# Window attention: the order of maxima and low halves, and shared value products for the previous chunk's keys

## The chip, the cores and the metric

One core of a Trainium2 chip runs one launch of the whole kernel. The metric is the device time of that launch in microseconds. The profile is of one further execution of the same program.

## The reference, cut to what matters

The program is one encoder block: projections with rotary positions, two attentions (a windowed one, A, and a differential one, B), gates and merge, a layer norm, and a mixture of experts. The change is in the windowed attention A alone. Its reference, for 2048 positions in chunks of 64, 8 query heads, 2 key heads, head size 64:

```python
qc = q.reshape(b, nc, CHUNK, A_KV_HEADS, grp, d)
kb = window_chunks(k, 2)   # keys of the chunk before and of the own chunk
vb = window_chunks(v, 2)
sc = einsum('bnqkgd,bnjkd->bnkgqj', qc, kb) * d ** -0.5
sc = where(valid, sc, NEG_INF)            # chunk 0 has no chunk before it
m = maximum(max(sc, -1), sink)            # one learned sink per head
e = exp(sc - m)
p = e / (sum(e, -1) + exp(sink - m))
o = einsum('bnkgqj,bnjkd->bnqkgd', p, vb)
```

## The kernel before, in words

The program runs in stages, each with a barrier behind it: weights and projection (j), differential attention (b), window attention (a, `window_attention_phase`, L480 to L770), merge (m), routing (r), experts (e), combination (o). Names of tiles in the profile carry the stage's letter: `a_tp` is `tp` of the window attention.

Float32 values are kept as a high part in fp32r and a low part, the remainder. So q and k are loaded as 64 rows of high parts on 64 rows of low parts; `kh` and `kl` hold the high and the low parts of the keys on both halves, and two products over 128 rows give all four terms.

A tile is 128 queries (two chunks). It needs 192 keys: the 64 of the chunk behind the tile and its own 128. A **unit** is one tile and one key head, which serves four query heads; there are UNITS = 32. In a unit the engines do this:

- TensorE, scores (L643 to L653): for each of 4 heads three products of 192 columns into a PSUM bank pair `bank[g]`: q with `kh`, q with `kl`, and a mask product that adds a large negative number where a chunk may not look. 12 matmuls.
- VectorE, maxima (L727 to L737): one reduction over the four heads' scores, then three small instructions up to `nb`, the negated maximum.
- ScalarE, exponentials (L698 to L703): four activations from PSUM into `pr` with their sums, and `se` for the sinks.
- TensorE, turn (L675 to L678): for each head two transposes of `pr`, the tile's own 128 keys into `tc` and the 64 behind it into `tp`. 8 matmuls. `tp` and `tc` are single buffers in PSUM.
- ScalarE copies them out as high parts `tph`, `tch` (L708, L709); VectorE makes the low halves `tpl`, `tcl` (L749, L751).
- TensorE, values (L655 to L669): for each head four products into `po[g]`, two over the tile's own 128 keys (128 and 64 columns) and two over the 64 keys behind it (64 and 128 columns; weights of 64 rows). 16 matmuls.
- VectorE scales by the inverse denominator (L744), GpSimd adds the two halves (L610), SP stores (L559). ScalarE and GpSimd also split one slice of the merge stage's weights a tile (L714, L603), which GpSimd's queue loads (L616).

The order of the work is written by hand, engine by engine. TensorE begins with the scores of units 0 and 1, and then in unit n does turn(n), scores(n+2), values(n-1). VectorE in unit n does the low halves of n, the inverse of n, maxima(n+2), and the scaling of n-1. ScalarE does copies(n), then exponentials(n+1). Four units are a turn of a loop (L626 to L634). turn(n) waits for the exponentials of n and, as `t_lo` starts at 2, for the low halves of n-1 (L672, L674). SP's queue loads q and k two tiles ahead, V one tile ahead, and stores (L561 to L585), in that order.

The core of TensorE's unit:

```python
pe.wait_ge(exped, n + 1)
pe.wait_ge(t_lo, 2 * n + 2)
# transposes of unit n
scores_of(k + u, 1 - u, g, 0)      # unit n + 2
values_of(n - 1, ...)
```

Of the kernel before, what the change touches and what calls it, by code (L numbers as in the profile page):

```python
# [21 lines left out]
P = 128  # L22
# [457 lines left out]
def window_attention_phase(nc, sinks, ident, qk_hi, qk_lo, v_hi, v_lo, oa, w_slices, w_hi, w_lo):  # L480
# [11 lines left out]
    UNITS = A_KV * NT  # L492
    with Phase(nc, "a") as ph:
# [18 lines left out]
        mask_f = ph.sb("mask_f", [P, P + 2 * W])  # L512
        mask = ph.sb("mask", [P, P + 2 * W], F32R)
        bank = [ph.ps(f"s{g}", [P, GH // 2, BANK]) for g in range(A_KV)]
        tp = ph.ps("tp", [CHUNK, GH, P])
# [7 lines left out]
        w_in, w_his, w_los = ph.sems("w_in", 2), ph.sem("w_his"), ph.sem("w_los")  # L523
        block = ph.block()

        def score(g, j):
            return bank[g][:, j // 2, (j % 2) * W:(j % 2 + 1) * W]

        @block.sync
        def _(sp):  # L530
            sp.dma_start(sink[:], sinks.rearrange("a (g h) -> a g h", g=A_KV).to_broadcast([P, A_KV, GH])).then_inc(sink_in, 16)
            for u in range(2):
                sp.sem_inc(stored[u], 16)


            def load_qk(t, u):
                cols = bass.ts(t, P)
                first = isinstance(t, int) and t == 0
                for half, src in ((0, qk_hi), (1, qk_lo)):
                    rows = slice(half * HD, (half + 1) * HD)  # L540
                    sp.dma_start(f(qs[rows, u]), src[0:4, :, cols].rearrange("c (b p) n -> p (c b) n", b=2)).then_inc(qk_loaded[u], 16)
                    for dst, ksrc in ((kh, qk_hi), (kl, qk_lo)):
                        k = ksrc[4].rearrange("(g p) n -> p g n", g=A_KV)
                        if first:
                            sp.dma_start(f(dst[rows, u, :, 0:CHUNK]), k[:, :, 0:CHUNK]).then_inc(stand_in, 16)
                            sp.dma_start(f(dst[rows, u, :, CHUNK:W]), k[:, :, cols]).then_inc(qk_loaded[u], 16)
                        else:
                            sp.dma_start(f(dst[rows, u]), k[:, :, bass.ds(t * P - CHUNK, W)]).then_inc(qk_loaded[u], 16)

            def load_v(t, u):  # L550
                first = isinstance(t, int) and t == 0
                tile, rows = (slice(0, 1), slice(0, CHUNK)) if first else (bass.ds(t - 1, 1), slice(CHUNK, P))
                for half, src in enumerate((v_hi, v_lo)):
                    for dst, at in ((vp, (tile, rows)), (vc, (bass.ds(t, 1), slice(0, P)))):
                        sp.dma_start(f(dst[:, u, :, half, :]), src[at[0], at[1], 0:A_K].rearrange("a p (g d) -> p (a g) d", g=A_KV)).then_inc(v_loaded[u], 16)

            def store(t, u):
                sp.wait_ge(added, 2 * t + 2)
                sp.dma_start(oa[bass.ts(t, P), :], o[:, u].rearrange("p g h d -> p (g h d)")).then_inc(stored[u], 16)  # L559

            def step(s, u):  # L561

                sp.wait_ge(scores, 2 * s + 2)
                load_qk(s + 2, u)

                sp.wait_ge(pv, 2 * s)
                load_v(s + 1, 1 - u)
                store(s - 1, 1 - u)

            load_qk(0, 0)  # L570
            load_v(0, 0)
            load_qk(1, 1)
            load_v(1, 1)
            sp.wait_ge(scores, 2)
            load_qk(2, 0)
            with sp.Fori(0, NT // 2 - 2) as i:
                step(2 * i + 1, 1)
                step(2 * i + 2, 0)
            step(NT - 3, 1)
            sp.wait_ge(pv, 2 * (NT - 2))  # L580
            load_v(NT - 1, 1)
            for t in range(NT - 3, NT):
                store(t, t % 2)
            for u in range(2):
                sp.wait_ge(stored[u], 16 * (NT // 2 + 1))  # L585

        @block.gpsimd
        def _(pool):


            nc.gpsimd.memset(mask_f[:], 0.0).then_inc(mask_step, 1)
# [3 lines left out]
            for first in range(2):  # L595
                m0 = P + W * first
                nc.gpsimd.memset(mask_f[0:1, m0 + P:m0 + W], NEG).then_inc(mask_step, 1)
                nc.gpsimd.memset(mask_f[32:33, m0:m0 + CHUNK], NEG).then_inc(mask_step, 1)
            nc.gpsimd.memset(mask_f[0:1, P + W:P + W + CHUNK], NEG).then_inc(mask_step, 1)
# [5 lines left out]
            def sum_parts(t):  # L605

                pool.wait_ge(stored[t % 2], 16 * (t // 2 + 1))
                for g in range(A_KV):
                    pool.wait_ge(scaled, 2 * t + g + 3)
# [13 lines left out]

        def over_tiles(eng, unit):  # L626
            for g in range(A_KV):
                unit(g, 0, 0, g, n0=True if g == 0 else False, tail=False)
            with eng.Fori(0, NT // 2 - 1) as i:
                for w in range(2):  # L630
                    for g in range(A_KV):
                        unit(2 * (2 * i + 1 + w) + g, i + w, 1 - w, g, n0=False, tail=False)
            for g in range(A_KV):
                unit(UNITS - 2 + g, NT // 2 - 1, 1, g, n0=False, tail=True)  # L634

        def tile_of(k, u):
            return 2 * k + u

        @block.tensor
        def _(pe):  # L640
            pe.wait_ge(mask_step, 9)

            def scores_of(k, u, g, first):  # L643

                if g == 0:
                    pe.wait_ge(qk_loaded[u], 6 * 16 * (k + 1))
                for j in range(GH):
                    q = qs[:, u, GH * g + j, :]
                    nc.tensor.matmul(score(g, j), q, kh[:, u, g, :], start=True, stop=False)
                    nc.tensor.matmul(score(g, j), q, kl[:, u, g, :], start=False, stop=False)  # L650
                    m0 = P + W * first
                    last = nc.tensor.matmul(score(g, j), mask[:, 0:P], mask[:, m0:m0 + W], start=False, stop=True)
                last.then_inc(scores, 1)  # L653

            def values_of(n, k, u, g):  # L655

                pe.wait_ge(t_lo, 2 * n + 4)

                pe.wait_ge(scaled, n + 1)
                if g == 0:  # L660
                    pe.wait_ge(v_loaded[u], 4 * 16 * (k + 1))
                for j in range(GH):

                    both, high = po[g][:, j].rearrange("p s d -> p (s d)"), po[g][:, j, 0, :]
                    nc.tensor.matmul(both, tch[:, g, j, :], vc[:, u, g].rearrange("p s d -> p (s d)"), start=True, stop=False)
                    nc.tensor.matmul(high, tcl[:, g, j, :], vc[:, u, g, 0, :], start=False, stop=False)
                    nc.tensor.matmul(high, tpl[:, g, j, :], vp[:, u, g, 0, :], start=False, stop=False)
                    last = nc.tensor.matmul(both, tph[:, g, j, :], vp[:, u, g].rearrange("p s d -> p (s d)"), start=False, stop=True)
                last.then_inc(pv, 1)  # L669

            def unit(n, k, u, g, n0, tail):
                pe.wait_ge(exped, n + 1)  # L672

                pe.wait_ge(t_lo, 2 * n + 2)  # L674
                for j in range(GH):  # L675
                    nc.tensor.transpose(tc[:, j, :], pr[:, g, j, CHUNK:W], ident[:])
                    last = nc.tensor.transpose(tp[:, j, :], pr[:, g, j, 0:CHUNK], ident[:])
                last.then_inc(turned, 1)  # L678
                if not tail:

                    scores_of(k + u, 1 - u, g, 0)
                if not n0:

                    if g:
                        values_of(n - 1, k, u, 0)
                    else:
                        values_of(n - 1, k - (1 - u), 1 - u, 1)


            pe.wait_ge(stand_in, 4 * 16)  # L690
            scores_of(0, 0, 0, 1)
            scores_of(0, 0, 1, 1)
            over_tiles(pe, unit)
            values_of(UNITS - 1, NT // 2 - 1, 1, 1)

        @block.scalar
        def _(act):
            def exps(n, g):  # L698
                act.wait_ge(maxed, 3 * n + 3)
                for j in range(GH):  # L700
                    nc.scalar.activation(pr[:, g, j, :], score(g, j), ACT.Exp, bias=nb[:, g, j:j + 1], scale=SCALE,
# [3 lines left out]
            def unit(n, k, u, g, n0, tail):  # L705

# [3 lines left out]
                if not (tail and g):  # L710
                    exps(n + 1, 1 - g)
                if g:
                    act.wait_ge(w_in[u], 16 * (k + 1))
                    nc.scalar.activation(w_hi[:, bass.ds(tile_of(k, u), 1), :], raw[:, u:u + 1, :], ACT.Copy).then_inc(w_his, 1)  # L714

            exps(0, 0)
            over_tiles(act, unit)

        @block.vector
        def _(dve):  # L720
            dve.sem_inc(t_lo, 2)
            dve.sem_inc(scaled, 2)
            dve.wait_ge(mask_step, 8)
# [3 lines left out]
            def maxima(n, g):  # L727
# [11 lines left out]
            def scale(n, k, u, g):  # L739
                dve.wait_ge(pv, n + 1)  # L740
                if not isinstance(n, int) or n >= 2:
# [5 lines left out]
            def unit(n, k, u, g, n0, tail):  # L747
                dve.wait_ge(t_hi, 2 * n + 1)
# [1509 lines left out]
```

## Time and profile before

| | |
|---|---|
| median of 3 runs | 3273.95 us (3270.92 to 3274.72) |
| profiled execution | 3276.61 us |
| its span, first to last instruction | 3275.1 us |
| mean granted TensorE clock | 0.898 |
| TensorE matmuls busy | 2722.8 us (83%) |
| VectorE busy | 1660.9 us (51%) |
| ScalarE busy | 1140.0 us (35%) |
| GpSimd busy | 794.2 us (24%) |
| window attention | 1400.27 to 1626.46 us of the span |

The profile is one execution. Times of instructions are counted from the span's start. PE is TensorE's matmuls and PEld its weight loads, which overlap them; DVE is VectorE, ACT ScalarE, POOL GpSimd, SP SyncE and SPq its queue of DMA issues. The end of a matmul in the profile is modelled, so its duration exceeds the time to the next one's start; the cost of one in a dense run is read from start to start. PEclk is the granted clock as a share of full speed, 2.4 GHz; its two levels are 1.0 and 0.5 (2.4 and 1.2 GHz), and a mean over a stretch lies between them. A bracket behind a row gives how long the engine had been idle, and what ended that.

### The profile page before, as it was taken

What the parts mean: (1) busy time and instruction counts of PE and PEld (TensorE: products, weight loads), DVE (VectorE), ACT (ScalarE), POOL (GpSimd) and SP (SyncE); (2) the same over time, 40 slices, a digit from 0 to 9 for tenths busy, and PEclk for the clock granted to TensorE, in tenths of its full rate; (3) what the DMA queues carried; (4) which work ended last, traced back from release to release, by engine and by line L of the source; (5) the groups of instructions that cost most, each with busy time, mean ns of one, the idle gap of its engine ahead of it and who ended that gap; (6) DMA issues with size and microseconds to landing.
All of it is one profiled execution on the core that took longest, in us unless ns stands there. A gap on an engine that the chain in (4) does not pass through costs nothing. (4 is left out here: it accounts for less than half of the span.)

```text
span 3275.1 us, 48737 instructions
## 1 busy us (share of the span) xinstructions
PE 2722.8 (83%) x14667; PEld 2336.4 (71%) x14668; DVE 1660.9 (51%) x3065; ACT 1140.0 (35%) x1888; POOL 794.2 (24%) x630
## 2 busy tenths in 40 slices
PE   2999993996978969889889997529999999999910
PEld 2888882885867858689778886317888888888810
DVE  5333332655636546345444443426565556666568
ACT  2111111433424434344311110216465455656522
POOL 2111110000000000023213232043343233324346
PEclk9999995997988979967699999759999999999965
DMA  4444437356373363355333331538687577768566
GB/s 148 144 144 144 144 132 184 109 157 178 118 213 122 134 186 134 112 150 139 102 119 119 105 119 41 182 116 326 240 303 283 215 285 282 285 234 314 212 222 220
DMA packets 278694, 582.78 MB, mean 178 GB/s; under 512 B 41536, under 2 KB 136000, under 8 KB 275520
## 3 DMA queue, kind: packets, MB, share of 16 engines
q1 hardware_dynamic: 184464, 437.26, 39.9%
q10 hardware_dynamic: 76944, 88.62, 7.7%
q0 software_dynamic: 17184, 55.60, 5.3%
q8 instruction: 57, 0.93, 0.1%
q14 instruction: 45, 0.37, 0.0%
HBM read 451.31 MB, written 130.07 MB: 178 GB/s over the span
## 5 line engine op out<-in xcount | busy, mean ns | idle before, releaser
L1776 DVE TENSOR_TENSOR e_wl<-rw_raw,e_wh 128x1024 fp32r<-128x1024 f32 (+1 forms) x288 | 374.2, 1343 | 46.4 <-ACT e_wh L1922 46.4
L1922 ACT ACTIVATE e_wh<-rw_raw 128x1024 fp32r<-128x1024 f32 (+1 forms) x384 | 377.9, 1053 | 17.3 <-DMA rw_raw<-w_gate_up 13.3
L1776 POOL TENSOR_TENSOR e_wl<-rw_raw,e_wh 128x1024 f32 (+1 forms) x96 | 238.8, 2512 | 298.2 <-ACT e_wh L1922 298.1
L301 PE MATMUL j_pg<-qkv_w_hi,j_xh 128*128 128x512 f32 (+1 forms) x640 | 242.4, 379 | 1.5 <-DVE j_xl L419 1.5
L303 PE MATMUL j_pg<-qkv_w_lo,j_xh 128*128 128x512 f32 (+1 forms) x640 | 237.3, 371 | 0.0
L302 PE MATMUL j_pg<-qkv_w_hi,j_xl 128*128 128x512 f32 (+1 forms) x640 | 236.4, 369 | 0.0
L1871 PE MATMUL e_p_up<-e_wh,e_xh 128*128 128x256 f32 (+1 forms) x784 | 225.4, 288 | 0.0
L1873 PE MATMUL e_p_up<-e_wl,e_xh 128*128 128x256 f32 (+1 forms) x784 | 221.7, 283 | 0.0
L1872 PE MATMUL e_p_up<-e_wh,e_xl 128*128 128x256 f32 (+1 forms) x784 | 221.7, 283 | 0.0
L931 POOL TENSOR_TENSOR b_o<-b_parts 128x128 f32<-128x128 f32 x64 | 30.9, 482 | 758.3 <-ACT b_parts L1044 758.3
L983 PE MATMUL b_pg<-b_g_wh,b_g_xh 128*128 128x512 f32 x512 | 213.6, 417 | 1.4 <-DVE b_g_out L1158 0.8
L1106 DVE TENSOR_SCALAR_CACHE_REDUCE b_sc<-b_s 128x512 f32<-128x512 f32 (+3 forms) x320 | 179.4, 605 | 49.2 <-PE b_s L958 36.1
L983 PE MATMUL b_pg<-b_g_wl,b_g_xh 128*128 128x512 f32 x512 | 203.5, 398 | 0.0
L983 PE MATMUL b_pg<-b_g_wh,b_g_xl 128*128 128x512 f32 x512 | 202.2, 395 | 0.0
L1036 ACT ACTIVATE b_th<-b_t 128x512 fp32r<-128x512 f32 (+3 forms) x160 | 85.3, 533 | 290.8 <-PE b_t L968 290.8
L955 PE MATMUL b_s<-b_kh,b_qs 128*128 128x512 f32 (+3 forms) x320 | 134.7, 421 | 55.0 <-issue 29.4
L1029 ACT ACTIVATE b_sc<-b_sc,b_nb 128x128 f32<-128x128 f32 (+15 forms) x128 | 153.0, 1195 | 54.1 <-DVE b_nb L1117 54.1
L1883 PE MATMUL e_py<-e_wh,e_hh 128*128 128x512 f32 x392 | 164.2, 419 | 0.0
L356 POOL TENSOR_TENSOR j_turned<-j_by_cos,j_by_sin 128x512 f32<-128x512 f32 x64 | 68.8, 1086 | 391.7 <-DVE j_by_sin L443 391.7
L968 PE MATMUL b_t<-ident,b_at 128*128 128x128 f32 x544 | 90.3, 282 | 86.0 <-DVE b_at L1139 86.0
L1871 PE MATMUL e_p_gate<-e_wh,e_xh 128*128 (+1 forms) x392 | 155.1, 396 | 5.9 <-DVE e_wl L1776 3.1
L438 DVE TENSOR_TENSOR j_by_cos<-j_pg,qkv_cos 128x512 f32<-128x512 f32 x64 | 37.7, 589 | 234.0 <-DMA v_lo<-j_vl 145.3
(313 smaller groups left out, 7307.6 us busy)
## 6 DMA issues: line engine op xcount, KB each, us to landing
rw_raw<-w_gate_up SPq DMA_DIRECT2D x256, 512.0 KB, 6.4
rw_raw<-w_down SPq DMA_DIRECT2D x128, 512.0 KB, 7.9
b_g_xh<-xt_hi SPq DMA_DIRECT2D x64, 512.0 KB, 4.0
b_g_xl<-xt_lo SPq DMA_DIRECT2D x64, 512.0 KB, 5.0
ys<-e_yo ACTq DMA_DIRECT2D x49, 512.0 KB, 7.6
gates<-b_g_out ACTq DMA_DIRECT2D x64, 256.0 KB, 4.4
m_gt<-gates SPq DMA_DIRECT2D x16, 1024.0 KB, 8.1
qk_hi<-j_qkh ACTq DMA_DIRECT2D x16, 832.0 KB, 4.5
```

The lines of the kernel that those rows point to most:

```text
L301: nc.tensor.matmul(out, xh[:, u, ks], w_hi[:, k, cs], start=(k == 0), stop=False)
L302: nc.tensor.matmul(out, xl[:, u, ks], w_hi[:, k, cs], start=False, stop=False)
L303: last = nc.tensor.matmul(out, xh[:, u, ks], w_lo[:, k, cs], start=False, stop=(k == KD - 1))
L983: last = nc.tensor.matmul(pg[:], x_side, w_side, start=(q == 0), stop=(q == PASSES - 1))
L1029: nc.scalar.activation(sc[:, u, m, 0:L], sc[:, u, m, 0:L], ACT.Exp, bias=nb[:, u, m:m + 1], scale=SCALE, accum_out=sums[:, u, m:m + 1]).th ...
L1106: nc.vector.tensor_scalar(sc[:, u, m, ks], bank[n % 4][:, 0:ks.stop - ks.start], 1.0, NEG, ALU.mult, ALU.max, accum_out=mx[:, u, m, g:g + ...
L1776: (nc.gpsimd if done is w_lo_pool else nc.vector).tensor_tensor(wl[:, slot(e, s), :], raw[:, s:s + 1, :], f(wh[:, slot(e, s), :]), ALU.sub ...
L1871: nc.tensor.matmul(out[:, 0:js.stop - js.start], xh[:, at], hi, start=(k == 0), stop=False)
L1872: nc.tensor.matmul(out[:, 0:js.stop - js.start], xl[:, at], hi, start=False, stop=False)
L1873: last = nc.tensor.matmul(out[:, 0:js.stop - js.start], xh[:, at], lo, start=False, stop=(k == KD - 1))
L1883: nc.tensor.matmul(py[:, js], hh[:, at], wh[:, n, js], start=(k == 0), stop=False)
L1922: nc.scalar.activation(wh[:, slot(e, s), :], raw[:, s:s + 1, :], ACT.Copy).then_inc(w_hi, 1)
```

## The change

TensorE now issues, in unit n, scores(n+1), turn(n), values(n-1), and the scores of 0 and 1 ahead of all. VectorE issues inverse(n-1), maxima(n+1), low halves(n-1), scaling(n-2). ScalarE issues exponentials(n+1), then copies(n). `pr` holds two heads side by side so that the 64 keys behind the tile of an even and of an odd head are neighbours: one transpose turns both (2 instead of 4 for `tp`), and one pair of products over 128 rows, against `vz`, whose rows hold V of those 64 keys twice with zeros elsewhere, gives both heads' part (256 columns). For that layout the scores of even heads are written in swapped pieces of 128 and 64 columns. The loops over tiles are written out.

```diff
-        vp = ph.sb("vp", [CHUNK, 2, A_KV, 2, HD], F32R)
+        vz = ph.sb("vz", [P, 2, A_KV, 2, 2, HD], F32R)
-        pr = ph.sb("pr", [P, A_KV, GH, W])
-        tph = ph.sb("tph", [CHUNK, A_KV, GH, P], F32R)
-        tpl = ph.sb("tpl", [CHUNK, A_KV, GH, P], F32R)
+        pr = ph.sb("pr", [P, A_KV, PAIRS, 2 * W])
+        tph = ph.sb("tph", [P, A_KV, PAIRS, P], F32R)
+        tpl = ph.sb("tpl", [P, A_KV, PAIRS, P], F32R)
-        tp = ph.ps("tp", [CHUNK, GH, P])
+        tp = ph.ps("tp", [P, PAIRS, P])
...
+            def load_qk(t):
+                u, cols = t % 2, slice(t * P, (t + 1) * P)
+                if t >= 2:
+                    sp.wait_ge(scores, 2 * t - 2)
...
+            def load_v(t):
+                u = t % 2
+                if t >= 2:
+                    sp.wait_ge(pv, 2 * t - 2)
...
                 for half, src in enumerate((v_hi, v_lo)):
+                    rows = tail[half][:, 0:A_K].rearrange("p (g d) -> p g d", g=A_KV)
+                    for j in range(2):
+                        sp.dma_start(f(vz[j * CHUNK:(j + 1) * CHUNK, u, :, j, half, :]), rows).then_inc(v_loaded[u], 16)
+                    sp.dma_start(f(vc[:, u, :, half, :]), src[t, :, 0:A_K].rearrange("p (g d) -> p g d", g=A_KV)).then_inc(v_loaded[u], 16)
...
+            load_qk(0)
+            sp.wait_ge(v_zeroed, 1)
+            load_v(0)
+            load_qk(1)
+            load_v(1)
+            for t in range(NT):
+                if t + 2 < NT:
+                    load_qk(t + 2)
+                if t and t + 1 < NT:
+                    load_v(t + 1)
+                if t:
+                    store(t - 1)
+            store(NT - 1)
...
         @block.gpsimd
         def _(pool):
+            nc.gpsimd.memset(f(vz[:]), 0.0).then_inc(v_zeroed, 1)
             nc.gpsimd.memset(mask_f[:], 0.0).then_inc(mask_step, 1)
...
         @block.tensor
         def _(pe):
+            def scores_of(n):
+                t, g = n // 2, n % 2
+                u, m0 = t % 2, P + M * (t == 0)
                 if g == 0:
+                    pe.wait_ge(qk_loaded[u], 6 * 16 * (t // 2 + 1))
+                if n >= 2:
+                    pe.wait_ge(exped, n - 1)
                 for j in range(GH):
+                    q, odd = qs[:, u, GH * g + j, :], j % 2
+                    nc.tensor.matmul(score(g, j), mask[:, 0:P], mask[:, m0 + odd * P:m0 + odd * P + W], start=True, stop=False)
+                    if odd:
+                        nc.tensor.matmul(score(g, j), q, kh[:, u, g, :], start=False, stop=False)
+                        last = nc.tensor.matmul(score(g, j), q, kl[:, u, g, :], start=False, stop=True)
+                    else:
+                        for k in (kh, kl):
+                            nc.tensor.matmul(score(g, j)[:, 0:P], q, k[:, u, g, CHUNK:W], start=False, stop=False)
+                            nc.tensor.matmul(score(g, j)[:, P:W], q, k[:, u, g, 0:CHUNK], start=False, stop=(k is kl))
                 last.then_inc(scores, 1)
+            def turn(n):
+                g = n % 2
+                pe.wait_ge(exped, n + 1)
+                if n:
+                    pe.wait_ge(t_lo, 2 * n)
+                for j in range(PAIRS):
+                    nc.tensor.transpose(tp[:, j, :], pr[:, g, j, P:2 * P], ident[:])
+                for j in range(GH):
+                    last = nc.tensor.transpose(tc[:, j, :], here_of(g, j), ident[:])
+                last.then_inc(turned, 1)
+            def values_of(n):
+                t, g = n // 2, n % 2
+                u = t % 2
+                pe.wait_ge(t_lo, 2 * n + 2)
+                if n >= 2:
+                    pe.wait_ge(scaled, n - 1)
                 if g == 0:
+                    pe.wait_ge(v_loaded[u], 6 * 16 * (t // 2 + 1))
+                here, there = vc[:, u, g].rearrange("p s d -> p (s d)"), vz[:, u, g].rearrange("p h s d -> p (h s d)")
+                for pair in range(PAIRS):
+                    both = po[g][:, 2 * pair:2 * pair + 2].rearrange("p h s d -> p (h s d)")
+                    nc.tensor.matmul(both, tph[:, g, pair, :], there, start=True, stop=False)
+                    nc.tensor.matmul(both, tpl[:, g, pair, :], there, start=False, stop=False)
+                    for j in (2 * pair, 2 * pair + 1):
+                        out = po[g][:, j].rearrange("p s d -> p (s d)")
+                        nc.tensor.matmul(out, tch[:, g, j, :], here, start=False, stop=False)
+                        last = nc.tensor.matmul(out, tcl[:, g, j, :], here, start=False, stop=bool(j % 2))
                 last.then_inc(pv, 1)
             pe.wait_ge(stand_in, 4 * 16)
+            scores_of(0)
+            scores_of(1)
+            for n in range(UNITS):
+                if 2 <= n + 1 < UNITS:
+                    scores_of(n + 1)
+                turn(n)
+                if n:
+                    values_of(n - 1)
+            values_of(UNITS - 1)
...
         @block.scalar
         def _(act):
+            exps(0)
+            for n in range(UNITS):
+                if n + 1 < UNITS:
+                    exps(n + 1)
+                copies(n)
+                if n % 2:
+                    k = n // 2
+                    act.wait_ge(w_in[k % 2], 16 * (k // 2 + 1))
+                    nc.scalar.activation(w_hi[:, k, :], raw[:, k % 2, :], ACT.Copy).then_inc(w_his, 1)
         @block.vector
         def _(dve):
+            def lows(n):
+                g = n % 2
+                dve.wait_ge(t_hi, 2 * n + 2)
+                nc.vector.tensor_tensor(tpl[:, g], tp[:], f(tph[:, g]), ALU.subtract).then_inc(t_lo, 1)
+                nc.vector.tensor_tensor(tcl[:, g], tc[:], f(tch[:, g]), ALU.subtract).then_inc(t_lo, 1)
+            maxima(0)
+            for n in range(UNITS):
+                if n:
+                    invert(n - 1)
+                if n + 1 < UNITS:
+                    maxima(n + 1)
+                if n:
+                    lows(n - 1)
+                if n >= 2:
+                    dve.wait_ge(summed, 2 * (n - 1))
+                    scale(n - 2)
+            invert(UNITS - 1)
+            lows(UNITS - 1)
+            dve.wait_ge(summed, 2 * UNITS)
+            scale(UNITS - 2)
+            scale(UNITS - 1)
```

The mask grows by one more block of 128 columns for each of its two forms, for the swapped pieces. GpSimd's and SP's waits for sums and stores count the same events with other offsets. The reduction, the exponentials and the scaling keep their shapes.

## Rows read from the trace of the kernel before

**Rows 1.** The page's busy time of TensorE, its weight loads and the other engines.
```profile
PE 2722.8 (83%) x14667; PEld 2336.4 (71%) x14668; DVE 1660.9 (51%) x3065; ACT 1140.0 (35%) x1888; POOL 794.2 (24%) x630
```

**Rows 2.** Stretches; columns: length, five engines' busy us (instructions), PEclk, DMA share, GB/s.
```profile
1400.00:1627.00 227.00, 223.63 (x1152) 203.86 (x1152) 113.67 (x288) 103.58 (x368) 67.20 (x62) 0.69 0.46 123
1440.00:1600.00 160.00, 160.00 (x844) 146.13 (x843) 83.02 (x211) 75.06 (x268) 50.10 (x46) 0.71 0.52 136
1600.00:1620.00 20.00, 20.00 (x84) 17.61 (x83) 8.02 (x19) 8.48 (x26) 6.37 (x6) 0.52 0.19 63
744.00:788.00 44.00, 19.14 (x68) 16.34 (x69) 17.45 (x64) 12.12 (x31) 2.00 (x4) 0.50 0.82 224
```

**Rows 3.** Order of time, the stage's start; columns: start us, duration us, engine, instruction.
```profile
1387.64 0.53 POOL L591 MEMSET a_mask_f<- 128x512 f32 x1 [7.97 <-POOLq L76]
...
1400.27 0.50 PE L649 MATMUL a_s<-a_kh,a_qs 128*128 128x192 f32 x1 [22.83 <-DMA a_kl<-qk_lo]
...
1402.70 0.41 PE L652 MATMUL a_s<-a_mask 128*128 128x192 f32 x1
...
1405.26 0.41 PE L652 MATMUL a_s<-a_mask 128*128 128x192 f32 x1
...
1405.71 0.96 DVE L729 TENSOR_REDUCE a_mx<-a_s 128x4 f32<-128x768 f32 x1 [1.05 <-PE a_s L652]
...
1406.29 0.21 ACT L703 ACTIVATE a_se<-a_diff 128x4 f32<-128x4 f32 x1
...
1406.56 0.48 PE L676 MATMUL a_tc<-ident,a_pr 128*128 128x128 f32 x1 [0.88 <-ACT a_se L703]
...
1406.98 0.16 DVE L737 TENSOR_SCALAR a_nb<-a_m 128x4 f32<-128x4 f32 x1
```

**Rows 4.** Order of time, the stage's last scaling.
```profile
1625.77 0.69 DVE L744 TENSOR_TENSOR a_parts<-a_o,a_inv 128x512 f32<-128x512 f32 x1 [4.03 <-PE a_o L668]
```

**Rows 5.** Waits in the stage; columns: who for whom, us in total, times, longest.
```profile
ACT a_tph L708 <- PE a_tp L677: 110.3, 32, 5.2
```

**Rows 6.** Order of time, two score products after the clock rose.
```profile
1410.11 0.27 PE L650 MATMUL a_s<-a_kl,a_qs 128*128 128x192 f32 x1
...
1410.22 0.27 PE L652 MATMUL a_s<-a_mask 128*128 128x192 f32 x1
```

**Rows 7.** Order of time, PE in the merge stage: two products of 512 columns.
```profile
1646.94 0.63 PE L1293 MATMUL m_psa<-mw_w_lo,m_abh 128*128 128x512 f32 x1
1647.37 0.63 PE L1291 MATMUL m_psa<-mw_w_hi,m_abh 128*128 128x512 f32 x1
```

**Rows 8.** Order of time, PE: a head's first value product and the next head's.
```profile
1516.76 0.33 PE L665 MATMUL a_o<-a_vc,a_tch 128*128 128x128 f32 x1
...
1517.47 0.33 PE L665 MATMUL a_o<-a_vc,a_tch 128*128 128x128 f32 x1
...
1604.70 0.47 PE L665 MATMUL a_o<-a_vc,a_tch 128*128 128x128 f32 x1
...
1605.88 0.47 PE L665 MATMUL a_o<-a_vc,a_tch 128*128 128x128 f32 x1
```

**Rows 9.** Groups by form in the stage; mean ns of one after the comma.
```profile
L749 DVE TENSOR_TENSOR a_tpl<-a_tp,a_tph 64x512 fp32r<-64x512 f32 x32 | 21.8, 682 | 44.5 <-ACT a_tph L708 44.5
L751 DVE TENSOR_TENSOR a_tcl<-a_tc,a_tch 128x512 fp32r<-128x512 f32 x32 | 21.5, 672 | 0.0
...
L753 DVE TENSOR_TENSOR a_den<-a_sums,a_se 128x4 f32<-128x4 f32 x32 | 4.6, 144 | 0.0
```

**Rows 10.** Waits of SP's queue in the stage.
```profile
SPq L555 <- PE a_o L668: 80.2, 14, 10.1
```

**Rows 11.** Order of time, PE in the routing stage, transposes alone.
```profile
2058.01 3.65 PE L1550 MATMUL r_pt<-ident,r_xin 128*128 128x128 f32 x16 [0.76 <-DVE r_tl L1631]
2062.41 1.07 PE L1550 MATMUL r_pt<-ident,r_xin 128*128 128x128 f32 x8 [0.76 <-DVE r_tl L1631]
```

**Rows 12.** Order of time, PE in the merge stage, after a gap.
```profile
1663.88 1.07 PE L1284 MATMUL m_pt<-ident,m_pa 128*128 128x128 f32 x8 [3.03 <-POOL m_pa L1376]
```

More of the change, by code:

```diff
@@ L492, in window_attention_phase @@
     UNITS = A_KV * NT
+    PAIRS = GH // 2
+    M = W + P
     with Phase(nc, "a") as ph:
@@ L511, in window_attention_phase @@
         raw = ph.sb("raw", [P, 2, D])
-        mask_f = ph.sb("mask_f", [P, P + 2 * W])
-        mask = ph.sb("mask", [P, P + 2 * W], F32R)
+        mask_f = ph.sb("mask_f", [P, P + 2 * M])
+        mask = ph.sb("mask", [P, P + 2 * M], F32R)
         bank = [ph.ps(f"s{g}", [P, GH // 2, BANK]) for g in range(A_KV)]
-        tp = ph.ps("tp", [CHUNK, GH, P])
+        tp = ph.ps("tp", [P, PAIRS, P])
         tc = ph.ps("tc", [P, GH, P])
@@ L531, in _ @@
             sp.dma_start(sink[:], sinks.rearrange("a (g h) -> a g h", g=A_KV).to_broadcast([P, A_KV, GH])).then_inc(sink_in, 16)
[L532 to L538, printed above, removed]
+            def load_qk(t):
+                u, cols = t % 2, slice(t * P, (t + 1) * P)
+                if t >= 2:
+                    sp.wait_ge(scores, 2 * t - 2)
                 for half, src in ((0, qk_hi), (1, qk_lo)):
@@ L543, in load_qk @@
                         k = ksrc[4].rearrange("(g p) n -> p g n", g=A_KV)
-                        if first:
+                        if t == 0:
                             sp.dma_start(f(dst[rows, u, :, 0:CHUNK]), k[:, :, 0:CHUNK]).then_inc(stand_in, 16)
@@ L547, in load_qk @@
                         else:
[L548 to L552, printed above, removed]
-                for half, src in enumerate((v_hi, v_lo)):
-                    for dst, at in ((vp, (tile, rows)), (vc, (bass.ds(t, 1), slice(0, P)))):
-                        sp.dma_start(f(dst[:, u, :, half, :]), src[at[0], at[1], 0:A_K].rearrange("a p (g d) -> p (a g) d", g=A_KV)).then_inc(v_loaded[u], 16)
@@ L573, in _ @@
[L573 to L583, printed above, removed]
+                            sp.dma_start(f(dst[rows, u]), k[:, :, t * P - CHUNK:(t + 1) * P]).then_inc(qk_loaded[u], 16)
@@ L595, in _ @@
             for first in range(2):
[L596 to L599, printed above, removed]
+                m0 = P + M * first
+                nc.gpsimd.memset(mask_f[0:1, m0 + CHUNK:m0 + P], NEG).then_inc(mask_step, 1)
+                nc.gpsimd.memset(mask_f[0:1, m0 + W + CHUNK:m0 + M], NEG).then_inc(mask_step, 1)
+                nc.gpsimd.memset(mask_f[32:33, m0 + P:m0 + W], NEG).then_inc(mask_step, 1)
+            nc.gpsimd.memset(mask_f[0:1, P + M + P:P + M + W], NEG).then_inc(mask_step, 1)
             def low_w(n):
@@ L621, in _ @@
             sum_parts(NT - 1)
[L626 to L634, printed above, removed]
@@ L647, in scores_of @@
                 for j in range(GH):
[L648 to L652, printed above, removed]
-                last.then_inc(scores, 1)
-            def values_of(n, k, u, g):
-                pe.wait_ge(t_lo, 2 * n + 4)
-                pe.wait_ge(scaled, n + 1)
-                if g == 0:
[L661 to L668, printed above, removed]
-                last.then_inc(pv, 1)
@@ L671, in unit @@
[L671 to L687, printed above, removed]
@@ L700, in exps, with copies @@
                 for j in range(GH):
-                    nc.scalar.activation(pr[:, g, j, :], score(g, j), ACT.Exp, bias=nb[:, g, j:j + 1], scale=SCALE,
+                    nc.scalar.activation(pr[:, g, j // 2, (j % 2) * W:(j % 2 + 1) * W], score(g, j), ACT.Exp, bias=nb[:, g, j:j + 1], scale=SCALE,
                                          accum_out=sums[:, g, j:j + 1])
                 nc.scalar.activation(se[:, g, :], diff[:, g, :], ACT.Exp).then_inc(exped, 1)
-            def unit(n, k, u, g, n0, tail):
+            def copies(n):
+                g = n % 2
@@ L709, in unit, with maxima @@
                 nc.scalar.activation(tch[:, g], tc[:], ACT.Copy).then_inc(t_hi, 1)
[L710 to L717, printed above, removed]
+            exps(0)
[7 more added lines that the diff above has]
+                    nc.scalar.activation(w_hi[:, k, :], raw[:, k % 2, :], ACT.Copy).then_inc(w_his, 1)
         @block.vector
         def _(dve):
-            dve.sem_inc(t_lo, 2)
-            dve.sem_inc(scaled, 2)
-            dve.wait_ge(mask_step, 8)
+            dve.wait_ge(mask_step, 10)
             nc.vector.tensor_copy(mask[:], mask_f[:]).then_inc(mask_step, 1)
             dve.wait_ge(sink_in, 16)
-            def maxima(n, g):
+            def maxima(n):
+                g = n % 2
                 dve.wait_ge(scores, n + 1)
@@ L745, in scale, with invert @@
                                         inv[:, g, :].unsqueeze(2).to_broadcast([P, GH, 2 * HD]), ALU.mult).then_inc(scaled, 1)
-            def unit(n, k, u, g, n0, tail):
-                dve.wait_ge(t_hi, 2 * n + 1)
-                nc.vector.tensor_tensor(tpl[:, g], tp[:], f(tph[:, g]), ALU.subtract).then_inc(t_lo, 1)
-                dve.wait_ge(t_hi, 2 * n + 2)
-                nc.vector.tensor_tensor(tcl[:, g], tc[:], f(tch[:, g]), ALU.subtract).then_inc(t_lo, 1)
+            def invert(n):
+                g = n % 2
                 dve.wait_ge(exped, n + 1)
@@ L755, in unit @@
                 nc.vector.reciprocal(inv[:, g, :], den[:, g, :]).then_inc(summed, 1)
[L756 to L768 removed]
+            def lows(n):
+                g = n % 2
+                dve.wait_ge(t_hi, 2 * n + 2)
[9 more added lines that the diff above has]
+                    lows(n - 1)
+                if n >= 2:
+                    dve.wait_ge(summed, 2 * (n - 1))
+                    scale(n - 2)
+            invert(UNITS - 1)
+            lows(UNITS - 1)
             dve.wait_ge(summed, 2 * UNITS)
[L770 removed]
+            scale(UNITS - 2)
+            scale(UNITS - 1)
 def diff_attention_phase(nc, w_in, b_gate, xt_hi, xt_lo, gates, lambdas, ident, qk_hi, qk_lo, v_hi, v_lo, ob):
```

54 lines of the change are left out of this document (16 added, 38 removed).

## The prediction

> **What bounds the kernel now.** The page comes first: over the span TensorE is busy 83% [rows 1], but a share of the span doesn't price an edit in one stage. The edit is in the window-attention stage alone, so the stretches are read next [rows 2]. The stage lasts from 1400.27 us, when TensorE (PE) starts on its first scores after waiting for a DMA [rows 3], to the end of the last scaling at 1626.46 [rows 4]: 226.2 us for 32 units, one for each tile and key head. From 1440 to 1600 PE is busy all 160 us, VectorE (DVE) half of them; PEclk is 0.71, so the clock alternates: x of the time full with 0.5(1-x)+x=0.71, x=0.42. The view of waits agrees: ScalarE waits 110.3 us for transposes [rows 5], and PE waits for nobody but at the start. PE's matmuls, and the clock they are granted, set this stage.
>
> So I price matmuls by start-to-start times. At half clock 12 score products of 192 columns start between 1402.70 and 1405.26 [rows 3]: 0.2133 us each. At full clock one takes 0.11 [rows 6]. 512 columns take 0.43 at half clock [rows 7], 0.84 ns a column, which makes 0.16 for 192: below 256 columns the instruction counts, its columns don't. One head's four value products take 1.18 us at half clock and 0.71 at full [rows 8], against 4x0.2133=0.85 and 0.44 by that price. The surplus of about 0.3 us comes with the two changes per head between weights of 128 rows and of 64.
>
> **The change, part by part.** Times are at half clock, then full.
> - Value products: 4 heads x 1.18 = 4.72 become 12 instructions, all on 128 rows, x 0.2133 = 2.56: -2.16 (full: 2.84 to 1.32, -1.52). 256 columns take 0.21 by 0.84 ns a column, the same.
> - Transposes: 8 become 6: -0.43 (-0.22).
> - Scores: 12 become 16, as the even heads' keys are written in two pieces for each of kh and kl: +0.85 (+0.44).
> Together -1.74 us a unit (-1.30): 32 units would give back 42 to 56 us. A unit has 34 matmuls, the stage 1088.
>
> **The new wait.** In unit n PE now issues scores(n+1), turn(n), values(n-1). turn(n) waits for the low halves of n-1, since tp and tc are single buffers. DVE issues those behind maxima(n+1), and these wait for scores(n+1), which PE has only just done. So in each unit PE stands from the end of its scores until DVE has made maxima and low halves. Behind turn(n) on PE's queue stand the value products and all that follows, and ScalarE's copies wait for the transposes. (Its new wait for the exponentials of two units back costs nothing: they are done a unit earlier.) Before, scores ran two units ahead and covered that work. The length of the wait: from the start of the last score product to the reduction 0.45 (1405.26 to 1405.71), less its own 0.21: 0.24; reduction to the end of nb 1.43 (1405.71 to 1407.14); low halves: between 144 ns for 4 columns and 682 for 512 the shorter tpl of 256 lies at 0.41, plus 0.67 for tcl, less 0.07 of overlap: 1.01; to PE 0.06, as from the end of se at 1406.50 to the transpose at 1406.56 [rows 3, 9]. Sum 2.74; units 1 to 30 have it: 82.5 us. Bounds: 2.6 if tpl's hop is shorter, 3.0 with two semaphore steps more: 4 us less or 8 more in all.
>
> **What stays hidden.** Each tile loads V with 6 DMAs for 4, 32 more on SP's queue, ahead of the stores and the next loads; SP spent 80.2 us waiting for value products before it might load V [rows 10], which covers them, and without that cover each would cost its issue, under a microsecond. POOL clears vz ahead of the mask: 1024 columns at 0.53 for 512 [rows 3] put the mask 1.1 us later, while PE waits for its DMA until 1400.27 anyway. ScalarE has about 3.3 us of work a unit, DVE under 4, below the period of 6 to 10. [...]
>
> **The sum, and the clock.** All at half clock: 1088 x 0.2133 = 232.1, plus 82.5, plus 2 for both ends: 317 us. All at full: 119.7+82.5+2 = 204. Before: 226. The clock decides. The rows show it at 0.52 from 1600 to 1620, where PE never rested but had come to the last units, which issue no scores any more, and at 0.50 from 744 to 788, where PE was busy 19 us of 44 [rows 2]. Before the change no unit had a gap, and still full clock held 42% of the time; now PE stands 2.74 of each 10.0 us (7.25+2.74). I take half clock, except that 6 of 32 units get their scores at full: 6x16x0.103 = 10 us less, 307. That is 80.4 above 226.2. The profiled execution took 3276.6 us, so 3357; the median shown is 2.7 lower: **3354**. This case spans 3325 (18 more units with fast scores) to 3362.
>
> **Rivals.** (B) Half clock throughout: 317, +90.4, 3364. It needs transposes, six in a row at the start of each busy run, to do nothing for the clock. Against it: sixteen transposes take 3.65 us and then, with only transposes behind them, eight take 1.07: the clock rose on transposes alone [rows 11]. The Trainium skill (TensorE: Matmul & The Clock Gate, Part 4: PE-mode transpose) says full clock doesn't engage for transposes; here it did. For B stands the gap.
> (C) The mix of before holds while PE works: 0.42 of the time at 0.11, 0.58 at 0.2133 is 0.153 us a matmul; 166.5+82.5+2 = 251, +25, 3299. For it: value products are denser without the row changes.
> (D) The other side: full clock throughout, 204, -22, **3252**. For it: after 3.03 us of idleness in the merge stage eight transposes still took 1.07 [rows 12]. Against: that followed long products of 512 columns; nothing so dense is here. It decides from 0.130 us a matmul, (226.2-84.5)/1088, so with four matmuls in five at full clock it is no slower.
> (E) Products cost their columns alone: 2304 in scores, 768 in transposes and 2048 in value products, 5120 a unit at 0.84 ns, 4.3 us; 138+82.5+2 = 222, -4, 3270. Against it: 192 columns took 0.2133 [rows 3]. The same skill page (Back-to-back issue gap) has the isolated gap as columns over 1.2 GHz at half clock; by that the narrow products would cost 0.05 to 0.11 us and the stage would end near this figure. The rows differ, and the sum goes by them.
> That the wait isn't there would need another order of the queues; the diff leaves none.
>
> **Numbers.** A .65, B .15, C .10, D .08, E .02. The time is A's. The range takes in A, B with the longer wait, and the ground toward C: 3310 to 3370; C, D and E, 0.20, are left out. A measurement of this kernel can tell about 0.2%, 6.5 us, from no change: faster is D, same is E, the rest is slower.
>
> **What would show it.** PE idle some 80 us in the stage, put down to tcl's low halves before the transposes; 36 matmuls a unit become 34; DVE waits for scores in every unit; a period near 10 us; PEclk under 0.6; a stage of 300 us. Value products at 0.21 apart at half clock show the row changes gone. The prediction is wrong if the transposes start with no gap behind the scores, or if the stage's PEclk is 0.7 or more.

## The result, and the profile after

The changed kernel takes 3350.5 us in the median of 4 runs (3348.4 to 3358.7), the kernel before 3272.4 (also of 4): a ratio of 1.0243, 95% interval 1.023 to 1.0256. It is slower by 78 us; 3354 was forecast. The profiled execution took 3350.23 us, 73.6 more than that of before.

The page of the changed kernel, its span, its busy time and the clock in 40 slices:

```profile
span 3348.7 us, 48040 instructions
...
PE 2716.8 (81%) x14603; PEld 2344.4 (70%) x14604; DVE 1647.3 (49%) x3065; ACT 1137.1 (34%) x1888; POOL 796.3 (24%) x633
...
PEclk9999996998979979755579999858999999999965
```

PE is busy 6 us less in all [rows 1], and slices 17 to 21, of 84 us each, read 7, 5, 5, 5, 7 for the clock; the stage covers the middle three and parts of the other two. The whole stage and its middle (columns as in [rows 2]):

```profile
1398.00:1706.00 308.00, 224.27 (x1088) 217.84 (x1088) 100.45 (x288) 100.82 (x368) 67.95 (x64) 0.54 0.37 96
1440.00:1600.00 160.00, 118.36 (x569) 115.21 (x570) 51.80 (x149) 53.15 (x195) 35.17 (x33) 0.53 0.40 105
```

The stage lasts from its first score at 1398.48 to 1700.2, the end of the last scaling: 301.7 us for 226.2. PE is busy 224.3 us in it where it was 223.6, with 64 matmuls fewer (1088 for 1152): the shapes' whole gain has gone into the slower clock, 0.54 for 0.69. In the middle PE is busy 118 us of 160, where it was busy all 160. The idle time is in the view of waits:

```profile
DVE a_mx L731 <- PE a_s L646: 201.3, 32, 11.8
ACT a_pr L702 <- DVE a_nb L739: 193.2, 32, 26.2
...
PE a_tp L660 <- DVE a_tcl L761: 76.1, 30, 2.5
...
ACT a_tph L709 <- PE a_tc L662: 26.1, 31, 2.9
```

PE waits 76.1 us for tcl's low halves, 30 times, up to 2.5 us; before, no such line was there. ScalarE's wait for the transposes has shrunk from 110.3 us [rows 5] to 26.1: it now waits for nb, which waits for scores. One such wait in order of time:

```profile
1520.91 0.41 PE L681 MATMUL a_o<-a_vc,a_tch 128*128 128x128 f32 x1
...
1521.12 0.41 PE L682 MATMUL a_o<-a_vc,a_tcl 128*128 128x128 f32 x1
...
1522.93 0.33 PEld L650 LDWEIGHTS a_s<-a_kh,a_qs 128*128 128x128 f32 x1
1523.04 0.36 PE L650 MATMUL a_s<-a_kh,a_qs 128*128 128x64 f32 x1
1523.15 0.33 PEld L649 LDWEIGHTS a_s<-a_kl,a_qs 128*128 128x128 f32 x1
...
1525.87 0.41 PE L646 MATMUL a_s<-a_kl,a_qs 128*128 128x192 f32 x1
...
1526.32 0.96 DVE L731 TENSOR_REDUCE a_mx<-a_s 128x4 f32<-128x768 f32 x1 [6.74 <-PE a_s L646]
...
1527.59 0.16 DVE L739 TENSOR_SCALAR a_nb<-a_m 128x4 f32<-128x4 f32 x1
1527.66 0.41 DVE L760 TENSOR_TENSOR a_tpl<-a_tp,a_tph 128x256 fp32r<-128x256 f32 x1
...
1527.99 0.68 DVE L761 TENSOR_TENSOR a_tcl<-a_tc,a_tch 128x512 fp32r<-128x512 f32 x1
...
1528.82 0.66 PE L660 MATMUL a_tp<-ident,a_pr 128*128 128x128 f32 x2 [2.54 <-DVE a_tcl L761]
```

Two value products stand 0.21 us apart at half clock, all on 128 rows. Around the product of 64 columns the starts of products are uneven, but the weight loads (PEld) stand 0.21 to 0.22 us apart there too. The last score starts at 1525.87, the reduction 0.45 later, nb ends at 1527.75, tcl at 1528.67, and the transposes start at 1528.82. The 2.54 us of idleness are counted from the modelled end of that score product, 0.41 us after its start; its slot is 0.21, so from start to start PE stands for 2.95-0.21 = 2.74 us, and by that the loss over 30 units is 82 us where the view says 76.1. The period of a unit at half clock is read from the starts of the transposes:

```profile
1662.65 0.66 PE L660 MATMUL a_tp<-ident,a_pr 128*128 128x128 f32 x2 [2.54 <-DVE a_tcl L761]
...
1672.62 0.66 PE L660 MATMUL a_tp<-ident,a_pr 128*128 128x128 f32 x2 [2.54 <-DVE a_tcl L761]
...
1682.59 0.66 PE L660 MATMUL a_tp<-ident,a_pr 128*128 128x128 f32 x2 [2.54 <-DVE a_tcl L761]
```

It is 9.97 us; 10.0 was forecast.

### The profile page after: what moved, and what is told of

Its sections match the earlier page's. It is cut to its first block and busy times, and to the rows that moved or that the text cites. A ratio compares the mean times of both kernels' runs of the same rounds, so it can differ in the third digit from the quotient of the medians.

```text
span 3348.7 us, 48040 instructions
## 1 busy us (share of the span) xinstructions
PE 2716.8 (81%) x14603; PEld 2344.4 (70%) x14604; DVE 1647.3 (49%) x3065; ACT 1137.1 (34%) x1888; POOL 796.3 (24%) x633
## 5 line engine op out<-in xcount | busy, mean ns | idle before, releaser
L1893 PE MATMUL e_py<-e_wl,e_hh 128*128 128x512 f32 x392 | 154.9, 395 | 0.0
```

Source lines behind the costliest of these rows:

```text
L1893: last = nc.tensor.matmul(py[:, js], hh[:, at], wl[:, n, js], start=False, stop=(k == KF - 1))
```

## The experiments

The theory: the new order makes PE stand 2.7 us a unit behind its own scores, and that keeps the clock at half. The rivals: the new shapes are slow in themselves; the clock fell for the kinds of products, not for the gap.

**Low halves ahead of maxima.** Two lines of VectorE's order are exchanged; all else is the changed kernel.

```diff
                 if n:
                     invert(n - 1)
+                    lows(n - 1)
                 if n + 1 < UNITS:
                     maxima(n + 1)
-                if n:
-                    lows(n - 1)
```

> The changed kernel with one exchange: VectorE makes the low halves of unit n-1 before it waits for the scores of unit n+1. Theory (the wait behind the maxima is what costs, directly by 76 us of idleness and again by keeping the clock at half): the wait of the transposes for the low halves goes, the matmuls stay 34 a unit, and the clock is at full for most of the stage. Stage 175 to 205 us instead of 302, total 3225 to 3255, faster than the kernel before. Rival 1 (the new shapes themselves are slow): total above 3330. Rival 2 (the wait goes but the clock stays at half): 1088 x 0.2133 = 232 us, total 3280.

Measured: 3246.7 us, ratio to the kernel before 0.9912 (0.9896 to 0.9929): 104 us below the change. Its middle of the stage, and its waits:

```profile
1440.00:1540.00 100.00, 84.93 (x564) 83.25 (x564) 56.80 (x146) 50.72 (x190) 36.74 (x34) 0.77 0.64 166
```

```profile
DVE a_tpl L760 <- ACT a_tch L710: 57.4, 32, 2.4
...
PE a_tp L660 <- DVE a_tcl L761: 29.5, 23, 2.5
```

PEclk is 0.77. The wait was forecast to go altogether; it is down from 76 us to 29.5 but not gone, as the low halves now wait for ScalarE's copies (57.4 us), which stand behind four exponentials. The kernel is faster than the one before, so the shapes aren't slow (rival 1), and the clock isn't at half (rival 2); the theory holds.

**The shapes alone.** PE, ScalarE and VectorE take up the order of the kernel before.

```diff
             for n in range(UNITS):
-                if 2 <= n + 1 < UNITS:
-                    scores_of(n + 1)
                 turn(n)
+                if n + 2 < UNITS:
+                    scores_of(n + 2)
                 if n:
                     values_of(n - 1)
...
```

> The shared transposes and value products alone, in the order of the kernel before: transposes n, scores n+2, values n-1; VectorE low halves n, inverse, maxima n+2, scaling n-1. Theory: no gap, 34 dense matmuls a unit. At half clock throughout the stage is 232 us and the total 3280; at full clock nearly throughout 145 us and 3190. Which of the two the clock takes I can't tell from the trace: half weight on each, both well under the 3350 of the change. Rival (the new shapes are slow in themselves): total above 3300, with value products or narrow scores further apart than 0.2133 us at half clock.

Measured: 3215.6 us, ratio 0.9821 (0.98 to 0.9841). Middle of the stage, and PE's wait:

```profile
1440.00:1540.00 100.00, 92.45 (x604) 91.74 (x604) 63.28 (x159) 54.10 (x206) 39.09 (x37) 0.74 0.68 187
```

```profile
PE a_s L643 <- DMA a_kl<-qk_lo: 8.4, 4, 3.4
```

The clock is neither full nor half but 0.74, so the time lies between the two figures and met neither. PE waits for low halves only once, 0.7 us at the stage's end; at this pace the loads of keys are late four times. The shapes save 60 us (the prediction had 42 to 56). This kernel and the change differ in the order alone, so with the new shapes the order costs 135 us: 82 of them are idleness of PE, and most of the rest is the clock, 0.53 for 0.74 in the middle.

**The order alone.** The changed kernel with the tiles, masks, V loads and products of before.

```diff
...
-                for j in range(PAIRS):
-                    nc.tensor.transpose(tp[:, j, :], pr[:, g, j, P:2 * P], ident[:])
                 for j in range(GH):
-                    last = nc.tensor.transpose(tc[:, j, :], here_of(g, j), ident[:])
+                    nc.tensor.transpose(tc[:, j, :], pr[:, g, j, CHUNK:W], ident[:])
+                    last = nc.tensor.transpose(tp[:, j, :], pr[:, g, j, 0:CHUNK], ident[:])
...
```

> The new order alone, with the transposes, value products, masks and V loads of the kernel before. Theory: the same gap, somewhat longer as the low halves are 64x512 and 128x512 (2.9 us, 87 us in all), and half clock nearly throughout: 32 x (20 x 0.2133 + 4.72) = 288, plus 87 and 3, is 378 us, total 3425. Rival (the order costs its gap alone and the clock keeps the mix of before): 226+87 = 313 us, total 3361. Rival (shapes are what costs): under 3300.

Measured: 3424.7 us, ratio 1.0462 (1.0445 to 1.048), on the theory's figure. Stretches, and the wait:

```profile
1398.00:1780.00 382.00, 290.49 (x1143) 256.09 (x1142) 108.95 (x288) 107.36 (x368) 68.00 (x64) 0.50 0.27 73
1440.00:1540.00 100.00, 75.32 (x298) 66.43 (x297) 29.31 (x78) 27.66 (x96) 17.21 (x16) 0.50 0.30 78
```

```profile
PE a_tc L651 <- DVE a_tcl L748: 83.9, 30, 2.8
```

The clock is 0.50 throughout. The order costs 149 us, of which 84 are idleness by this view (90 from start to start); the rest is the clock, 0.50 for 0.71. With the shapes' -60 that makes +89 where both together measured +78.

**The gap filled.** Idle transposes in the changed kernel, ahead of the wait; VectorE's work and the wait itself are as in the change.

```diff
                 pe.wait_ge(exped, n + 1)
+                if 1 <= n < UNITS - 1:
+                    for _ in range(12):
+                        nc.tensor.transpose(bank[g][:, 1, 2 * W:BANK], here_of(g, 0), ident[:])
                 if n:
                     pe.wait_ge(t_lo, 2 * n)
```

> The changed kernel with 12 idle transposes (of scores already turned, into a part of a PSUM bank that nobody reads) on TensorE's queue ahead of the wait for the low halves, in each of the 30 units that have the wait. At half clock they take 12 x 0.2133 = 2.56 us, as long as the gap; at full 1.3. Theory (the gap is what keeps the clock down): full clock nearly throughout, 1088 x 0.11 = 120 plus the waits 30 x 2.7 = 81 plus the ends, 205 to 212 us, total 3250 to 3262, below the kernel before although TensorE does 360 matmuls more and VectorE's wait is as long as ever. Rival (the clock falls for the shapes of the products, not for the gap): half clock stays, total 3350 to 3360.

Measured: 3262.0 us, ratio 0.9958 (0.994 to 0.9975). Middle of the stage, and PE's wait:

```profile
1440.00:1540.00 100.00, 81.79 (x709) 78.22 (x709) 48.89 (x142) 50.52 (x184) 34.68 (x32) 1.00 0.59 155
```

```profile
PE a_tp L662 <- DVE a_tcl L763: 34.1, 31, 1.1
```

One unit, from its transposes to the next ones, in order of time:

```profile
1499.23 0.44 PE L662 MATMUL a_tp<-ident,a_pr 128*128 128x128 f32 x2 [1.14 <-DVE a_tcl L763]
...
1502.96 0.28 PE L646 MATMUL a_s<-a_kl,a_qs 128*128 128x192 f32 x1
1503.08 1.47 PE L658 MATMUL a_s<-ident,a_pr 128*128 128x128 f32 x12
1505.69 0.44 PE L662 MATMUL a_tp<-ident,a_pr 128*128 128x128 f32 x2 [1.14 <-DVE a_tcl L763]
```

The clock is at 1.00. PE does 360 transposes more and the kernel is 88 us faster than the change, and 0.4% under the kernel before. From the last score (1502.96) to the transposes (1505.69) it is 2.73 us, 2.95 in the change; from the reduction's start to the end of tcl VectorE takes 2.35 us in both. But a unit takes 6.46 us for 9.97. This parts the two costs: the wait costs its own time, 2.7 us a unit, and the clock another 3.5. Not all of the 3.5 was lost to the gap: the run of the shapes alone, which hasn't this gap, had 0.74, so the idle transposes bring the clock higher than the order of before does.

**What fills it.** Six transposes instead of twelve, and twelve mask products in place of the transposes.

```diff
-                        nc.tensor.transpose(bank[g][:, 1, 2 * W:BANK], here_of(g, 0), ident[:])
+                        nc.tensor.matmul(bank[g][:, 1, 2 * W:BANK], mask[:, 0:P], mask[:, P:2 * P], start=True, stop=True)
```

> As the run with the filled wait with 6 transposes in place of 12, half of the gap at half clock. Theory: between the unfilled and the filled kernel, PEclk 0.75 to 0.95 in the stage, total 3265 to 3310. If the clock wants the gap closed altogether: 3340 to 3350. If any work in it does: 3262.

> As the run with the filled wait, but the 12 idle instructions are products of the mask with itself, 128 columns in fp32r, in place of transposes of float32. They take the same time on TensorE. If every instruction of the same length counts the same for the clock: 3262 as there. If transposes count for more: the clock is full only part of the time, PEclk 0.75 to 0.9 in the stage, total 3270 to 3300. If products of mostly zeros count for nothing: 3340 to 3355.

Measured: 3280.8 us (3274.6 to 3294.3) with six, 3280.0 (3267.2 to 3291.0) with products. The middle of the stage with six transposes, then with twelve products:

```profile
1440.00:1540.00 100.00, 73.13 (x577) 69.57 (x576) 46.94 (x135) 46.36 (x172) 30.95 (x29) 0.93 0.54 141
```

```profile
1440.00:1540.00 100.00, 87.46 (x627) 85.54 (x627) 43.85 (x126) 42.91 (x160) 27.55 (x27) 0.84 0.50 131
```

The clocks, 0.93 and 0.84, lie between the unfilled and the filled kernel, as expected. They don't rank the two fillings: the profiled execution was one of the shortest with six transposes (3275.0) and one of the longest with products (3289.3), and the medians are equal. With twelve the two kinds do differ: all runs with transposes (3260.4 to 3265.9) lie under all with products that take as long. Whether for being transposes of float32 or for the zeros in the mask wasn't parted.

**A longer wait.**

```diff
...
                 nc.vector.tensor_tensor(tpl[:, g], tp[:], f(tph[:, g]), ALU.subtract).then_inc(t_lo, 1)
+                nc.vector.tensor_tensor(spare[:, g], tc[:], f(tch[:, g]), ALU.subtract)
                 nc.vector.tensor_tensor(tcl[:, g], tc[:], f(tch[:, g]), ALU.subtract).then_inc(t_lo, 1)
```

> The changed kernel with one more subtraction of 128x512 on VectorE ahead of the low halves of tc, into a tile that nobody reads: 0.61 us more in each of the 30 waits. Theory (the wait is serial, nothing covers it): +18 us if the clock keeps its few stretches at full, up to +28 if it loses them all: total 3368 to 3380. Rival (part of the wait is covered by something else that is late too): under 3360.

Measured: 3375.9 us, ratio 1.031 (1.0289 to 1.0332). The wait:

```profile
PE a_tp L661 <- DVE a_tcl L763: 94.0, 30, 3.1
```

94.0 us for 76.1: the 18 us come through in full, and nothing covers the wait. The stage of the profiled execution lasts from 1399.99 to 1722.49, 322.5 us for 301.7; so about 3 us are left for the clock in it, and the rest of the 25 us between the medians lies outside the stage.

**Value products ahead of scores.** The run of the shapes alone with PE's order turn(n), values(n-1), scores(n+2).

> The new shapes with TensorE's order transposes n, value products n-1, scores n+2, and the other engines as in the kernel before. Value products and transposes, which the clock rose behind, now stand together, and scores stay two units ahead. Theory: no wait, full clock for most of the stage, 145 to 170 us for it, total 3190 to 3215. Rival (the loads of q and k, for which TensorE waited 8 us in the run of the shapes alone, take over): 3215 to 3230. Rival (the value products now wait for the low halves of their own unit's predecessor at once): over 3230.

Measured: 3214.3 us, ratio 0.9824 (0.9793 to 0.9855), at the upper end. The middle of the stage; a moment in it, GpSimd and VectorE in order of time; and two of VectorE's groups:

```profile
1440.00:1540.00 100.00, 90.24 (x667) 88.92 (x666) 75.26 (x184) 62.48 (x234) 44.13 (x41) 0.85 0.80 198
```

```profile
1473.82 2.38 POOL L608 TENSOR_TENSOR mw_w_lo<-a_raw,mw_w_hi 128x1024 fp32r<-128x1024 f32 x1 [1.40 <-ACT mw_w_hi L720]
...
1474.33 1.88 DVE L736 SCALAR_TENSOR_TENSOR a_m<-a_mx,a_sink 128x4 f32<-128x4 f32 x1
...
1476.25 0.16 DVE L738 TENSOR_TENSOR a_diff<-a_sink,a_m 128x4 f32<-128x4 f32 x1
```

```profile
L736 DVE SCALAR_TENSOR_TENSOR a_m<-a_mx,a_sink 128x4 f32<-128x4 f32 x32 | 24.7, 773 | 1.1
...
L753 DVE TENSOR_TENSOR a_den<-a_sums,a_se 128x4 f32<-128x4 f32 x32 | 4.8, 151 | 0.0
```

The clock is 0.85, and something new binds: the small instruction L736, 161 ns elsewhere, takes 1.88 us and ends at 1476.21, when GpSimd's subtraction ends (1476.20). It reads two operands from SBUF. In 32 units it costs 24.7 us where 5.2 would do. It holds up `nb`, the exponentials behind it, and through them PE, which stands before its transposes 12 times:

```profile
PE a_tp L660 <- ACT a_se L704: 15.7, 12, 3.1
```

**Its operands in PSUM.** mx and m, four columns each, move into a spare part of the score bank.

```diff
+        def small(g, i):
+            return bank[g][:, 1, 2 * W + GH * i:2 * W + GH * (i + 1)]
...
-                nc.vector.scalar_tensor_tensor(m[:, g, :], mx[:, g, :], SCALE, sink[:, g, :], ALU.mult, ALU.max).then_inc(maxed, 1)
+                nc.vector.scalar_tensor_tensor(small(g, 1), small(g, 0), SCALE, sink[:, g, :], ALU.mult, ALU.max).then_inc(maxed, 1)
...
```

> The run of value products ahead of scores, with the maxima (mx) and their scaled values (m), four columns each, kept in PSUM in a spare part of the score bank. In that run one small VectorE instruction with both operands in SBUF took up to 1927 ns in place of 161, each time as long as GpSimd's 2.4 us subtraction ran. Theory (VectorE's instructions with two operands from SBUF wait for GpSimd's SBUF access, those with one from PSUM don't): this instruction takes 165 ns everywhere, the 19.5 us of its surplus go, 10 to 19 of them from the stage: total 3195 to 3205. Rival (the stall moves on to the next instruction of two SBUF operands, the sum of the denominators, or the stage is bound by ScalarE): 3208 to 3216.

> The same two tiles in PSUM in the run of the shapes alone (scores ahead of value products). Its stage takes 167 us with PEclk 0.74 in the middle and 8 us of waits for the loads of q and k; its small instruction was held up too, up to 1637 ns. If the hold-ups were on its path: 3200 to 3210. If the clock and the loads bind it: 3212 to 3218, no change.

Measured: 3203.1 us, ratio 0.9773 (0.9759 to 0.9786), for the first, the fastest of all; 3215.9 (3205.9 to 3230.0), ratio 0.9803, for the second, no change. VectorE's same groups in the first (L739 was L736, L756 was L753), and its middle of the stage:

```profile
L756 DVE TENSOR_TENSOR a_den<-a_sums,a_se 128x4 f32<-128x4 f32 x32 | 10.3, 322 | 0.0
...
L739 DVE SCALAR_TENSOR_TENSOR a_s<-a_s,a_sink 128x4 f32<-128x4 f32 x32 | 5.5, 170 | 1.1
```

```profile
1440.00:1540.00 100.00, 93.86 (x717) 92.72 (x715) 71.41 (x191) 64.70 (x243) 45.38 (x43) 0.86 0.80 210
```

L739 takes 170 ns on the mean and 171 at most, and PE's waits for `se` are down to a single one of 1.4 us. Part of the stall has moved on: the sum of the denominators, which still reads two operands from SBUF, takes 322 ns for 151, and up to 750 while GpSimd adds the two halves. So the theory's time came, and from the rival the part that the stall moves on. Keeping `se` in PSUM as well wasn't tried. In the second run the median is that of the shapes alone (3215.6), as expected if the clock and the loads bind it; its five runs spread over 24 us, so a gain of a few us could hide in them.

## Why the prediction was right

- **What bounds the stage.** PE and its clock: confirmed by the filled gap, where more work on PE at a faster clock saved 88 us.
- **The shapes.** 34 matmuls a unit at 0.2133 and no surplus for row changes. The clearest figure is the period at half clock: 9.97-2.74 = 7.23 us of work for 34 matmuls, 0.213 each, where 7.25 was put. So on the mean products of 64 and 128 columns cost what those of 192 and 256 do, and rival E is out.
- **The new wait.** Forecast 2.74 us a unit, measured 2.74 from start to start. Two of its terms were off and cancel: tpl starts 0.09 us before nb ends (1527.66 against 1527.75), which the sum had one behind the other, and from tcl's end to the transposes it takes 0.15 us where 0.06 was put. So the exact agreement is luck, by a tenth of a microsecond. (30 x 2.74 is 82.2, where the prediction has 82.5.)
- **The clock.** Forecast: half, but for six units. Measured: PEclk 0.54 in the stage, and 29 distances between transposes of which 23 read 9.97 to within 0.01 and six 8.0 to 8.1. One of the six:

```profile
1423.02 0.66 PE L660 MATMUL a_tp<-ident,a_pr 128*128 128x128 f32 x2 [2.54 <-DVE a_tcl L761]
...
1431.09 0.66 PE L660 MATMUL a_tp<-ident,a_pr 128*128 128x128 f32 x2 [2.54 <-DVE a_tcl L761]
```

The gap as the cause of the low clock is borne out by the filled gap and by both pairs of kernels that differ in the order (the pair with the old shapes also in the written-out loops). The number six is luck: the prediction gives no working for it. One reading behind the forecast was loose. The prediction says that the units from 1600 to 1620 issue no scores any more; in the kernel before, scores still stand there, 0.21 us apart, up to this one:

```profile
1603.42 0.41 PE L652 MATMUL a_s<-a_mask 128*128 128x192 f32 x1
```

So the clock was at half there before the scores ended. B, half clock throughout, would have been 3364, 14 us over the measured time and within the range; the order alone did that (0.50). C needed the mix of before and D a clock of 1.00, which only the filled gap brought.

- **The sum.** 307 us for the stage, measured 301.7. The one term that was mis-sized is what full clock gives back, 10 us. The six units alone gave back 11.6, since a stretch at full clock takes in value products too; the other 4 of 317-301.7 = 15 lie at the two ends of the stage, where the last value products also ran at full clock. The stage is 75.5 us longer than before where 80.4 was forecast, and the profiled execution as a whole 73.6.
- **What was hidden stayed hidden.** V's extra loads, the clearing of vz and the written-out loops show in no wait of PE: the first score starts at 1398.48, behind a DMA of kl as before. That holds at the change's pace; in the faster runs the loads of keys were late a few times (8.4 us in the run of the shapes alone), and whether the extra loads of V have a part in that wasn't tested.

The Trainium skill (TensorE: Matmul & The Clock Gate, Part 4: PE-mode transpose) says that full clock doesn't engage for transposes. The runs differ for these transposes of float32: twelve in each gap, among the stage's products, held the clock at 1.00, where without them it was 0.53.

## What to carry to other kernels

When an in-order engine's work is moved ahead of something that another engine waits for, follow the ring: who waits for the moved work's input, and who has just produced it. Here a one-unit shift turned a covered step into a wait of 2.7 us a unit; exchanging two steps took 104 us off. On a bound TensorE price a gap twice, once for its length and once for the clock of the work around it; if it can't be closed, idle instructions in it may pay.

## What the runs showed of the hardware

- A gap of 2.7 us in each 9.97 took TensorE's clock in the middle of the stage to 0.53, where the same products without that gap had 0.74, with PE idle 7.5 us of 100 for late loads; with the shapes of before a gap of 3.0 us in 11.97 took it from 0.71 to 0.50. Filling the gap with twelve transposes brought 1.00, with six, which leave more than half of it idle, 0.93 in the profiled execution, with twelve products 0.84.
- The clock also fell where PE had no gap at all (0.71 before the change [rows 2]). Why is open: no run here settles it.
- Products of 64, 128, 192 and 256 columns and transposes of 128 share one slot, 0.213 us at half clock on the mean of a unit's 34; the weight loads, one for each product, stand that far apart even where the products' own starts are uneven.
- A VectorE instruction of four columns with two operands from SBUF was held in 13 of 32 units, for up to 1.93 us, while GpSimd subtracted 1024 columns in SBUF; with one operand in PSUM it took 0.17 in all 32. The Trainium skill (SBUF — State Buffer, SBUF: two separate sides) states a lock between the two engines for VectorE instructions with two SBUF inputs against a GpSimd instruction that reads SBUF; the runs agree.
